# Two blocks of a model on one core: three heads' results and the small columns are loaded during the last scan, and the first output weights are split ahead of the first head's product

## The reference

```python
def step(state, inp):                       # scan over chunks, for each of 16 heads
    ...
    o = jnp.einsum('bhcd,bhde->bhce', qd, state) + jnp.einsum('bhcs,bhse->bhce', qkc, v_new)
    ...
o = rms_norm(o, norm_w) * jax.nn.silu(z)    # per head of 128 channels
y = o.reshape(bsz, t, nh * dh) @ w_out      # 2048 x 1024
x = x + gate * y
return rms_norm(x, final_g)                 # first block; the second one norms it again (norm_pre)
```

## Time and profile before

| | |
|---|---|
| runs | 2102.33, 2098.05 and 2096.22 us, median 2098.05 us |
| profiled execution | 2098.08 us, of which the span is 2096.3 us |
| recurrence | to about 917 us of the span |
| output stage, first pass | 919 to about 1021 us |
| PE busy over the span | 1992.0 us (95%) |
| DVE, ACT busy | 1273.6 us (61%), 853.6 us (41%) |

### The profile page before, as it was taken

How to read it: one execution, slowest core, us unless ns; L and a number is a source line. 1 busy time by engine, 2 the same in 40 slices (tenths; PEclk the granted TensorE clock), 3 DMA queues, 4 the chain that set the end, 5 groups by cost and what they waited for, 6 DMA issues and landing times.

```text
span 2096.3 us, 29439 instructions
## 1 busy us (share of the span) xinstructions
PE 1992.0 (95%) x11256; PEld 1618.5 (77%) x11256; DVE 1273.6 (61%) x2417; ACT 853.6 (41%) x1377; POOL 138.0 (7%) x114
## 2 busy tenths in 40 slices
PE   5989999999999999969999999999999999999998
PEld 2667878888887888857776787777777678888877
DVE  6777878796869686749625644445353435633543
ACT  4644353544344443149403333535343337600321
POOL 0020202011111212000000000000000000000000
PEclk8999999999999999989999999999999999999999
DMA  7222323232323242548313221120312125211232
GB/s 279 90 76 70 98 78 106 66 101 72 104 68 102 70 121 67 170 148 284 91 43 138 67 66 36 46 95 21 111 41 81 61 79 213 91 50 42 87 114 81
DMA packets 128971, 200.27 MB, mean 96 GB/s; under 512 B 56596, under 2 KB 88084, under 8 KB 127808
## 3 DMA queue, kind: packets, MB, share of 16 engines
q1 hardware_dynamic: 128832, 198.39, 29.6%
HBM read 156.22 MB, written 42.11 MB: 95 GB/s over the span
## 4 chain that ended last, share of the span: by engine, by line
PE 47%; DVE 4%; DMA 2%; issue 2%; ACT 1%; SPq 0%; DVEq 0%; ACTq 0%
PE m_job L1710 6%; PE m_job L1712 6%; PE m_job L1711 6%; PE e_b L2397 4%; PE e_b L2398 4%; PE e_b L2399 4%; PE p_out L1359 2%; PE p_sc L1956 2%; PE p_out L1361 2%; PE p_out L1360 2%; PE p_s L1979 2%; PE e_b L2468 1%; PE e_b L2467 1%; PE e_b L2466 1%; DMA m_raw<-in_w 1%
## 5 line engine op out<-in xcount | busy, mean ns | idle before, releaser
L795 PE MATMUL p_job<-h_hi,w_hi 128*128 128x512 f32 x768 | 321.7, 419 | 18.2 <-DVE h_lo L185 16.8
L797 PE MATMUL p_job<-h_hi,w_lo 128*128 128x512 f32 x768 | 302.6, 394 | 0.0
L796 PE MATMUL p_job<-h_lo,w_hi 128*128 128x512 f32 x768 | 302.1, 393 | 0.0
L1710 PE MATMUL m_job<-h_hi,m_hi 128*128 128x512 f32 x576 | 237.7, 413 | 2.8 <-issue 2.1
L1712 PE MATMUL m_job<-h_hi,m_lo 128*128 128x512 f32 x576 | 227.1, 394 | 0.0
L1711 PE MATMUL m_job<-h_lo,m_hi 128*128 128x512 f32 x576 | 226.0, 392 | 0.0
L795 PEld LDWEIGHTS p_job<-h_hi,w_hi 128*128 128x128 f32 x768 | 146.0, 190 | 59.3 <-issue 16.4
L796 PEld LDWEIGHTS p_job<-h_lo,w_hi 128*128 128x128 f32 x768 | 145.9, 190 | 35.1 <-issue 7.9
L797 PEld LDWEIGHTS p_job<-h_hi,w_lo 128*128 128x128 f32 x768 | 145.6, 190 | 31.3
L1710 PEld LDWEIGHTS m_job<-h_hi,m_hi 128*128 128x128 f32 x576 | 108.8, 189 | 49.8 <-issue 28.3
L633 ACT ACTIVATE pre<-p_job 128x512 f32<-128x512 f32 x96 | 56.7, 591 | 177.6 <-PE p_job L797 174.9
(11 more groups left out here) (398 smaller groups left out, 4170.1 us busy)
## 6 DMA issues: line engine op xcount, KB each, us to landing
w_raw<-in_w SPq DMA_DIRECT2D x49, 512.0 KB, 3.6
m_raw<-in_w SPq DMA_DIRECT2D x49, 512.0 KB, 3.7
rows<-grows SPq DMA_DIRECT2D x32, 512.0 KB, 6.8
ada<-in_ada_w SPq DMA_DIRECT2D x8, 1024.0 KB, 5.3
z_scr<-pre SPq DMA_DIRECT2D x16, 512.0 KB, 2.6
o_scr<-oT SPq DMA_DIRECT2D x64, 128.0 KB, 1.8
ob<-o_scr SPq DMA_DIRECT2D x16, 512.0 KB, 4.9
zb<-z_scr SPq DMA_DIRECT2D x16, 512.0 KB, 4.9
```

Source lines behind the costliest of these rows:

```text
L795: nc.tensor.matmul(bank, hi, h_hi[:, k, cut], start=(k == 0), stop=False)
L796: nc.tensor.matmul(bank, hi, h_lo[:, k, cut], start=False, stop=False)
L797: last = nc.tensor.matmul(bank, lo, h_hi[:, k, cut], start=False, stop=(k == KD - 1))
L1710: nc.tensor.matmul(bank, hi, h_hi[:, k, cut], start=(k == 0), stop=False)
```

## The change

Five things are edited.

1. The three buffers of `ob` and one tile `out_cols` for the three small columns exist for the whole kernel, with their semaphores. The scratch reserved for another kind of dynamic DMA, which the kernel doesn't issue, is set to 1,024 bytes.
2. SP loads heads 0, 1 and 2 into `ob` and the three small columns at "merge" 0 of iteration 8. It waits there until the first two pairs' results are stored.
3. After the border SP begins with `zb` of head 0, then waits for the last result's store, and goes on as before with `ob` from head 3.
4. ACT loads the table with Exp and Ln in the last scan, behind the result of the last chunk but one, and no longer at the head of the output stage.
5. On DVE the split of head 0's weights is ahead of head 0's multiplication by `rinv`, and `low_square(2)` is behind head 0's low part.

```diff
@@ SP, iteration 8 of the recurrence
+                        elif s[0] == "merge" and not s[1] and i == QK_HEADS:
+                            for q in range(2):
+                                sp.wait_ge(o_stored[q], 16 * NT)
+                            for m in range(3):
+                                sp.dma_start(keep["ob"][:, m, :], io["o_scr"][m]).then_inc(keep["o_in"][m], 16)
+                            for at, n, src in ((0, 1, "norm_w"), (KD, KD, "final_g"), (2 * KD, KD, "norm_pre")):
+                                sp.dma_start(keep["out_cols"][:, at:at + n], io[src]).then_inc(keep["cols_in"], 16)
@@ ACT, "write" step of the scan
                             nc.scalar.activation(oT[:, c % 2], p_query, ACT.Copy).then_inc(o_done, 1)
+                            if m == NT * QK_HEADS - 2:
+                                nc.scalar.preload_act_table_set(EXP_LN)
@@ SP, output stage
-            load_o(0)
-            load_o(1)
-            sp.wait_ge(keep["o_stored"], 16 * QK_HEADS * NT // 2)
-            for dst, src in ((nw, io["norm_w"]), (fg, io["final_g"]), (np_col, io["norm_pre"])):
-                sp.dma_start(dst[:], src).then_inc(cst, 16)
             for m in range(len(steps)):
                 if m < V_HEADS:
                     if m >= 3:
                         sp.wait_ge(ylo_done, m - 2)
                     sp.dma_start(zb[:, m % 3, :], io["z_scr"][m]).then_inc(z_in[m % 3], 16)
-                if 2 <= m + 1 < V_HEADS:
+                if m == 0:
+                    sp.wait_ge(keep["o_stored"], 16 * QK_HEADS * NT // 2)
+                if 3 <= m + 1 < V_HEADS:
                     load_o(m + 1)
@@ ACT, output stage
-            nc.scalar.preload_act_table_set(EXP_LN)
@@ DVE, output stage
             for m, (q, n) in enumerate(steps):
+                if m == 0:
+                    split(m)
                 if q == 0:
                     z = zb[:, n % 3, :]
                     dve.wait_ge(gz_done, n + 1)
                     dve.wait_ge(rinv_done, n + 1)
                     nc.vector.tensor_tensor(z, z, rinv[:], ALU.mult).then_inc(y_done, 1)
-                split(m)
+                if m:
+                    split(m)
                 if q == 0:
-                    if n + 2 < V_HEADS:
+                    if n and n + 2 < V_HEADS:
                         low_square(n + 2)
                     dve.wait_ge(yhi_done, n + 1)
                     nc.vector.tensor_tensor(y(1, n), z, y(0, n).bitcast(F32), ALU.subtract).then_inc(ylo_done, 1)
+                    if n == 0:
+                        low_square(2)
                     if n + 1 < V_HEADS:
                         gated(n + 1)
@@ build
+            "ob": sb("ob", [P, 3, T]), "out_cols": sb("out_cols", [P, 32]),
@@ kernel
-    nc = bacc.Bacc("TRN2", target_bir_lowering=False, num_devices=1)
+    nc = bacc.Bacc("TRN2", target_bir_lowering=False, num_devices=1, dynamic_dma_scratch_size=1024)
```

More of the change, by code:

```diff
@@ L1158, in stage_out @@
         w_lo = sb("wo_lo", [P, 2, W3], F32R)
-        ob = sb("ob", [P, 3, T])
+        ob, out_cols = keep["ob"], keep["out_cols"]
+        nw, fg, np_col = out_cols[:, 0:1], out_cols[:, KD:2 * KD], out_cols[:, 2 * KD:3 * KD]
         zb = sb("zb", [P, 3, T])
@@ L1164, in stage_out @@
         rinv = sb("rinv3", [P, T])
-        nw = sb("nw", [P, 1])
-        fg = sb("fg", [P, KD])
-        np_col = sb("np_col", [P, KD])
         fn = sb("fn", [P, KD])
@@ L1185, in y @@
             return middle[:, n - KD, :] if n < KD + 2 else high[:, n - KD - 2, :]
-        cst = sem("c_cst"); x_in = sem("c_x"); o_in = [sem(f"c_o{q}") for q in range(3)]; z_in = [sem(f"c_z{q}") for q in range(3)]
+        cst = keep["cols_in"]; x_in = sem("c_x"); o_in = keep["o_in"]; z_in = [sem(f"c_z{q}") for q in range(3)]
         sq_done = sem("c_sq"); sqhi_done = sem("c_sqhi"); sqlo_done = sem("c_sqlo"); ones_set = sem("c_ones"); ss_done = sem("c_ss"); ln_done = sem("c_ln"); rinv_done = sem("c_rinv")
@@ L2760, in build @@
             "o_stored": ctx.enter_context(nc.semaphore("o_stored")),
+            "o_in": [ctx.enter_context(nc.semaphore(f"o_in{q}")) for q in range(3)],
+            "cols_in": ctx.enter_context(nc.semaphore("cols_in")),
         }
```

## The result

The changed kernel took 2108.23 us (median of five runs, 2106.22 to 2111.47), the kernel before 2098.05 us (median of five, 2096.22 to 2102.33). The ratio is 1.0054 with an interval of 1.0043 to 1.0065: slower by 10 us, 0.5%, where 3.9 us of gain were forecast. The profiled execution of the changed kernel was the slowest of its five, 2111.47 us.

A forecast was written before the change was run, and what follows sets the result against it. PE, busy 95% of the span, was taken as the bound, so only its idle time at the border could be won. 3.75 + 0.21 - 0.11 = 3.85 us off 2098.08 us gave 2094.2 us, range 2092.2 to 2097.6 us.

The forecast's parts named there:

- Scratch size, tile addresses: Whole kernel: no instruction of the changed kernel uses the scratch, so its new size and the addresses cost 0.
- Rival G: Whole kernel: the change of addresses speeds or slows other operations; either sign, no size given; chance 0.03.
- The loads of `ob`: Border: loaded ahead of it at no cost, they let ACT square head 0 3.75 us earlier.
- The table load: Last scan: there it delays the last chunk's copy by 0.11 us; left at the border it would cost 1.28 us.
- Rival E: Last scan: the table load costs up to 1.4 us more on ACT between dependent chunks; 2095.6 us; chance 0.05.
- `zb`: Behind the border: head 0's load lands after 3.75 us; taken as 0, at worst 0.4 us late.
- Rival C: Behind the border: a late `zb` holds `gated(0)` until 925.8 us, 1.7 us lost; 2095.9 us; chance 0.07.
- The DVE order: Output stage, head 0: DVE's low part then waits only for ACT's high part; worth 0.21 us in the sum.
- The wait of head 2: First pass: DVE's wait for head 2's inverse root shrinks from 2.57 us to about 1.4 us.
- rival B: First pass: PE's clock rises at another moment; 2092.8 us if sooner, 2096.2 us if late; chance 0.14, either way.
- rival F: Before the border: `ob` loads slow the gate vector's last load; 2 us slower than before, 2100 us; chance 0.04.
- rival D: First pass: DMA transfers could be the real pace, so the gain is given back; 2098 us; chance 0.05.

The follow-up runs named there:

- `a1_scratch_only`: The kernel before with the scratch cut to 1,024 bytes and nothing else; 2096.5 us, ratio 0.9998 to the kernel before.
- `a3_cols_first`: The changed kernel with `out_cols` placed ahead of `h_hi` and `h_lo`, every instruction kept; 2090.06 us, ratio 0.9962 to the kernel before.

## Why the prediction was wrong, and where it was right

**The step that failed** is "Scratch size, tile addresses. No instruction of the changed kernel uses the scratch; I cost it at 0." The first half of the reason holds: the scratch alone costs nothing (`a1_scratch_only`). But the question asked was who uses the scratch, and not which tiles move against which. The edit put the two operands of 5,664 of the 11,256 products, those with `h_hi` or `h_lo`, at a distance that is no longer the old one plus a multiple of 256 bytes. The step from such a product to the next grew by some 5 ns, from 1235 to 1750 us by 2.4 ns. It cost 15.5 us, three to four times what the border gained. The prediction's own sign of being wrong, that the last scan starts late, was there: all is 5.2 us late at 907 us. Rival G named this, with 0.03 and no price; "either sign" was its whole content. The median, 2108.23 us, lies 10.6 us above the range.

**The loads of `ob`** were worth what the sum said. 3.82 us at the first sums, 3.75 forecast; 3.51 us when undone alone. Their issue was not as cheap as the sum had it: from the first of the three (880.66 us) to the end of the last column's (885.60 us) SP took 4.94 us and not 2.6. It had the time; the next store, at 898.78 us, is late by no more than all else, 5.2 us.

**The small columns** were, as forecast, the next wait if they stay behind: 0.76 us.

**The table load** in the scan cost 0.11 us, the term as put, and saves 1.28 us at the border. The Trainium skill (ScalarE: Activation LUTs, What ACT_TABLE_LOAD costs) adds a drain of about 1.38 us to each switch to another set of tables. This trace doesn't show it: 919.18 us is the end of the copy ahead, 919.20 us the load's start, 920.50 us the next copy. Rival E is out.

**`zb`** arrived as estimated: its load is issued at 924.36 us and `gated(0)` starts at 928.13 us, 3.77 us behind that, and delays nothing. Rival C is out.

**The DVE order** was worth 0.23 us by its own experiment; the term was 0.21.

**The wait of head 2** was forecast at 1.4 us and measured 0.33 us. That is 1.1 us more than the sum, and it is rival B in its favourable form, with 0.14 for B either way. The clock after:

```profile
939.00:940.00 1.00, 1.00 (x4) 0.77 (x3) 0.96 (x2) 0.70 (x1) 0.00 (x0) 0.50 0.48 164
940.00:941.00 1.00, 1.00 (x5) 0.81 (x4) 0.97 (x3) 0.70 (x1) 0.00 (x0) 0.75 0.68 209
```

The granted clock (the third number from the end) goes from 0.50 to full within the microsecond from 940 us, some 3.8 us after the first product, where before it took about 6. The sums for head 2 then run at 2.4 GHz. I don't claim this 1.1 us for the change; it is luck. In `a1_scratch_only`, whose instructions are those of before, the clock rises 4.0 us after the first product and the same wait is 1.56 us instead of 2.57:

```profile
945.19 1.23 DVE L1459 TENSOR_TENSOR zb<-zb,rinv 128x1024 f32<-128x1024 f32 x1 [1.56 <-ACT rinv L1275]
```

In the eight traces with the old border the rise comes 4.0 to 6.2 us after the first product, in `a3_cols_first` 4.4 us after it, with a wait of 0.61 us.

**The later load of the gate vector** (rival F, the slower one) did not occur; its user has its 1.69 us of slack. **The gain was not given back** in the first pass (rival D): 4.9 of the 5.2 us of head 2 are there at head 15.

## What to carry to other kernels

An edit that adds a tile or changes a reserved size moves every tile behind it. Before costing that at nothing, list the addresses of both operands of the hot products before and after, and see whether a distance changed by something that is no multiple of 256 bytes (changes by 32, 64 and 128 bytes over such a multiple were tried here, and all cost about the same, 4 to 5 ns a product); here a tile of 128 bytes in the wrong place cost 15 us and hid a gain of 4 to 5. And when a change disappoints, pair the two traces along the span first: a loss that grows ahead of the edited place is no matter of the edit's instructions.

## What the runs showed of the hardware that I had not expected

A product of 128 columns of weights with 512 columns (128x512) starts 227 to 228 ns after the one before at the distances tried that are a multiple of 256 bytes (69,632, 69,888, 70,144 and 81,920 bytes from `h_hi` to `w_hi`), and 232.6 to 233.2 ns after it at 69,664, 69,696, 69,760 and 82,048 bytes. This holds whichever side `h_hi` is on: streamed in `e_b<-h_hi,m_hi`, weights in `e_b<-y_hi,h_hi`. The Trainium skill (TensorE: Matmul & The Clock Gate, Step-by-step: what each phase is for) says that PE has two independent read ports, one for the streamed operand and one for weight loads, and that loading weights takes no read bandwidth from a running product. These runs don't show which two reads meet, or that any do; they show that the two operands' places are not without effect on each other. Open are the cause, other distances and tile shapes, and why the products between 1235 and 1750 us take 230 ns a step with the distance of before too, against 232.4 ns with the changed one, so that there the placement costs only half as much.
